# Hybrid SSD/MLA/PEER layer on one core: the modulation slabs' sums one unit later with two accumulators, TensorE's scan loop written out, and block 0's closing norm placed among block 1's expert rows

## The reference, cut to what matters

```python
ada = silu(c) @ w_ada + b_ada                       # (1, 6 * 2048), the modulation vector
shift1, scale1, gate1, shift2, scale2, gate2 = split(ada, 6)
h = layer_norm(x) * (1 + scale1) + shift1
z, xbc, dt_raw, q_a, kv_a, k_r, g_logits = split(h @ w_in)
y_ssd = ssd_branch(z, xbc, dt_raw, ...)             # 8 groups of 8 heads, scan in chunks of 64
y_mla = mla_branch(q_a, kv_a, k_r, ...)             # 16 heads, then one projection w_mla_out
mix = (g0 * y_ssd + g1 * y_mla) @ w_mix_out
x = post_layer_norm(ALPHA * x + (1 + gate1) * mix)
h2 = layer_norm(x) * (1 + scale2) + shift2
f = peer_ffn(h2, ...)                               # per token 8 heads x 16 experts of 16384
return post_layer_norm(ALPHA * x + (1 + gate2) * f)
```

## Time and profile before

| | us |
|---|---|
| median of 3 runs | 2916.93 (2910.3 to 2918.87) |
| the profiled execution's own time | 2912.79 |
| its span, first to last instruction | 2911.1 |
| TensorE busy | 2407.8 (83%) |
| DVE busy | 2123.8 (73%) |
| ACT busy | 982.4 (34%) |
| GpSimd busy | 881.9 (30%) |
| mean granted TensorE clock | 0.908 |
| mla, first to last matmul of its units | 424 to 533 |
| scan, eight groups | 535 to 1110 |
| last value row added | 2882.2 |

### The profile page before, as it was taken

The page is one execution under the profiler, slowest core; times in us unless marked ns, Lnnn a source line. Parts: engine busy times, 40 slices in busy tenths (PEclk is TensorE's granted clock), DMA queues, the critical chain, the costliest instruction groups (busy, mean ns, idle before and its releaser), DMA issues.

```text
span 2911.1 us, 38817 instructions
## 1 busy us (share of the span) xinstructions
PE 2407.8 (83%) x14598; PEld 2031.0 (70%) x14598; DVE 2123.8 (73%) x2562; ACT 982.4 (34%) x1337; POOL 881.9 (30%) x725
## 2 busy tenths in 40 slices
PE   4589998999999999999869766665565679999990
PEld 3589998988888888999759765665565664444440
DVE  7766667788878785444565888888898796666568
ACT  1144442344444444433343222225767630000000
POOL 0000001122222220000100565665665715444343
PEclk9799999999999999999989887877777779999995
DMA  8755658756555564655544899998999929999995
GB/s 343 290 171 200 226 198 295 254 203 205 203 201 202 203 210 167 233 179 182 217 144 145 339 368 377 397 376 361 394 374 370 414 90 413 413 413 414 414 413 228
DMA packets 144961, 817.83 MB, mean 281 GB/s; under 512 B 16520, under 2 KB 21248, under 8 KB 70832
## 3 DMA queue, kind: packets, MB, share of 16 engines
q0 software_dynamic: 93200, 477.21, 42.1%
q1 hardware_dynamic: 49728, 336.05, 31.3%
q10 hardware_dynamic: 1888, 2.59, 0.2%
HBM read 811.55 MB, written 4.23 MB: 280 GB/s over the span
## 4 chain that ended last, share of the span: by engine, by line
PE 42%; DVE 21%; DMA 20%; issue 9%; POOL 4%; ACT 3%; ACTq 0%; DVEq 0%; POOLq 0%
DMA vrow<-in_p_vg,acc 11%; PE ps L653 10%; PE ps L655 9%; PE ps L654 9%; DMA rrow<-in_peer_u,acc 7%; DVE ps L2042 3%; DVE rrow L2013 3%; POOL rrow L2177 3%; DVE wlo L1464 2%; ACT whi L1058 2%; PE ps L633 2%; DVE acc L1513 2%; PE ps L634 2%; PE ps L635 2%; DVE oh L2055 1%
## 5 line engine op out<-in xcount | busy, mean ns | idle before, releaser
L1464 DVE TENSOR_TENSOR wlo<-raw,whi 128x2048 fp32r<-128x2048 f32 x216 | 506.8, 2348 | 374.5 <-ACT whi L1058 365.1
L1058 ACT ACTIVATE whi<-raw 128x2048 fp32r<-128x2048 f32 x216 | 412.7, 1913 | 704.6 <-PE ps L655 479.2
L2177 POOL DMA_INDIRECT rrow<-in_peer_u,acc x256 | 443.5, 1732 | 455.4 <-DVE acc L1961 202.8
L2013 DVE CUSTOM_DVE_ANT_0 rrow<-rrow,h 128x2048 f32<-128x2048 f32 x200 | 449.6, 2287 | 61.0 <-DMA rrow<-in_peer_u,acc 60.6
L653 PE MATMUL ps<-h_hi,whi 128*128 128x256 f32 (+1 forms) x1568 | 453.1, 289 | 5.1 <-DVE wlo L1464 3.9
L2042 DVE SCALAR_TENSOR_TENSOR ps<-vrow,acc,ps 128x1024 f32<-128x1024 f32 x254 | 327.1, 1288 | 164.4 <-DMA vrow<-in_p_vg,acc 143.5
L654 PE MATMUL ps<-h_lo,whi 128*128 128x256 f32 (+1 forms) x1568 | 443.4, 283 | 0.0
L655 PE MATMUL ps<-h_hi,wlo 128*128 128x256 f32 (+1 forms) x1568 | 443.4, 283 | 0.0
L2177 POOL DMA_INDIRECT vrow<-in_p_vg,acc x256 | 247.7, 968 | 321.7 <-DVE ps L2042 232.6
L653 PEld LDWEIGHTS ps<-h_hi,whi 128*128 128x128 f32 (+1 forms) x1568 | 299.0, 191 | 17.9 <-issue 9.3
L654 PEld LDWEIGHTS ps<-h_lo,whi 128*128 128x128 f32 (+1 forms) x1568 | 299.0, 191 | 4.0 <-issue 3.8
(11 more groups left out here) (336 smaller groups left out, 4430.1 us busy)
## 6 DMA issues: line engine op xcount, KB each, us to landing
raw<-in_p_in SPq DMA_DIRECT2D x104, 1024.0 KB, 4.9
ada_in<-in_p_ada POOLq DMA_DIRECT2D x128, 512.0 KB
vden<-in_p_vd SPq DMA_DIRECT2D x64, 1024.0 KB
ada_in<-in_p_ada SPq DMA_DIRECT2D x32, 1024.0 KB, 10.0
raw<-in_p_so SPq DMA_DIRECT2D x32, 1024.0 KB, 4.8
raw<-in_p_mo SPq DMA_DIRECT2D x16, 1024.0 KB, 6.9
raw<-in_p_bc SPq DMA_DIRECT2D x16, 1024.0 KB, 4.9
raw<-in_p_mix SPq DMA_DIRECT2D x16, 1024.0 KB, 4.8
```

Of the source, the lines that this page charges most:

```text
L1058: F(whi[:, n % 2, :, 0:cols_], raw[:, n % 4, :, 0:cols_], ACT.Copy).then_inc(hi_ready, 1)
L1464: V.tensor_tensor(wlo[:, n % 2, :, 0:cols_], raw[:, n % 4, :, 0:cols_], whi[:, n % 2, :, 0:cols_].bitcast(F32), ALU.subtract).then_inc(lo_ ...
L2013: last = V.tensor_tensor_reduce(row, row, h2[:, b, :], 1.0, 0.0, ALU.mult, ALU.add, dots[:, k, e:e + 1])
L2177: return G.indirect_dma_start(out=dst, out_offset=None, in_=table, in_offset=bass.IndirectOffsetOnAxis(ap=eid_all[:, r:r + 1], axis=0))
```

## The change

- mla is written out on TensorE and ACT and DVE, as four slabs. DVE fills accumulator `s % 2`; TensorE sums slab s-1 after the first unit of slab s, and DVE makes the row after `lo(4s+2)`. Only the last slab's sum stays right behind its own units. ACT's store and bias load go behind the second split of the slab.
- In the scan the accumulator is `g`; TensorE sums the group before after unit u, DVE makes its row after `lo(u+2)`. Quarter 2 of the modulation sum goes from between `lo(u+8)` and `lo(u+9)` to behind the masks `mt`, ahead of `lo(u+10)`. GpSimd's list is as before.
- TensorE's scan is written out in Python, all four pairs; DVE, ACT and GpSimd keep their loops.
- The last group's sum, row and store go into g0's first units.
- The end: `residual(b, c)` makes one half of a block's residual and its two statistics, `last_norm(b)` the norm in two halves. Block 0's two halves stand before rows 192 and 236, its norm before row 240, block 1's dense half before row 246 (rows counted from 0 to 255). After the last row are left block 1's gathered half, its moments and its norm. SP stores four pieces of 512 KB.

```diff
 # SP
-                    sp_.wait_ge(fin_ready, b + 1)
-                    sp_.dma_start(out[0, b * P:(b + 1) * P, :], fin[:, b, :]).then_inc(out_done, 16)
+                    for c in range(0, D, DV):
+                        sp_.wait_ge(fin_ready, 2 * b + c // DV + 1)
+                        sp_.dma_start(out[0, b * P:(b + 1) * P, c:c + DV], fin[:, b, c:c + DV]).then_inc(out_done, 16)
 # PE, mla
-                with pe.Fori(0, 2) as i:
-                    pe.wait_ge(row_ready, i * 2 + (ADA_MLA + 1))
-                    for s in range(2):
-                        for q in range(4):
-                            pe.wait_ge(o_split, q + 1)
-                            channel_unit(U_MLA, 4 * s + q, i, N_MLA, oT_hi, oT_lo, 4 * q, DC - 1, slab_tiles(1 - s))
-                        if s:
-                            pe.wait_ge(row_ready, i * 2 + (ADA_MLA + 2))
-                        sum_slab(aux[:, 0, :], 0, i * 2 + (ADA_MLA + s))
+                pe.wait_ge(row_ready, ADA_MLA + 1)
+                for s in range(4):
+                    for q in range(4):
+                        pe.wait_ge(o_split, q + 1)
+                        channel_unit(U_MLA, 4 * s + q, 0, 0, oT_hi, oT_lo, 4 * q, DC - 1, slab_tiles(1 - s % 2))
+                        if s and q == 0:
+                            if s > 1:
+                                pe.wait_ge(row_ready, ADA_MLA + s)
+                            sum_slab(aux[:, 0, :], (s - 1) % 2, ADA_MLA + s - 1)
+                pe.wait_ge(row_ready, ADA_MLA + 4)
+                sum_slab(aux[:, 0, :], 1, ADA_MLA + 3)
 # PE, scan
                             channel_unit(U_SSD, u + q, i, N_SSD, h_hi, h_lo, 4 * q, DC - 1, slab_tiles(bx))
+                            if q == 0 and grp:
+                                sum_slab(aux[:, 2, :], 1 - g, grp - 1 + ADA_SSD)
...
-                        sum_slab(aux[:, 2, :], 0, grp + ADA_SSD)
...
-                ssd_pair(0, True)
-                with pe.Fori(1, 4) as i:
-                    ssd_pair(i, False)
+                for i in range(4):
+                    ssd_pair(i, i == 0)
 # ACT, mla
+                for s in range(4):
+                    for q in range(4):
+                        hi(U_MLA, 4 * s + q + 2, 0, 0)
+                        if q == 1:
+                            if s:
+                                ada2_store(ADA_MLA + s - 1)
+                            ada2_bias(ADA_MLA + s)
+                ada2_store(ADA_MLA + 3)
 # DVE
-                    dve.wait_ge(acc_summed, slab + (QUARTERS + 2))
+                    two = in_ssd or isinstance(slab, int) and slab > ADA_MLA
+                    dve.wait_ge(acc_summed, slab + (QUARTERS + 2) - (1 if two else 0))
...
+                for s in range(4):
+                    for q in range(4):
+                        ada2(ADA_MLA + s, q, into=s % 2)
+                        lo(U_MLA, 4 * s + q + 2, 0, 0)
+                        if s and q == 0:
+                            ada2_row(aux[:, 0, :], ADA_MLA + s - 1)
+                    slab_done(U_MLA, 4 * s + 3, 0, 0)
...
                         lo(U_SSD, u + 2, i, N_SSD)
+                        if not (first and g == 0):
+                            ada2_row(aux[:, 2, :], slab - 1)
                         lo(U_SSD, u + 3, i, N_SSD)
...
                         lo(U_SSD, u + 8, i, N_SSD)
-                        ada2(slab, 2, True)
                         lo(U_SSD, u + 9, i, N_SSD)
...
+                        ada2(slab, 2, True, g)
                         lo(U_SSD, u + 10, i, N_SSD)
-                        ada2(slab, 3, True)
+                        ada2(slab, 3, True, g)
                         lo(U_SSD, u + 11, i, N_SSD)
...
-                        ada2_row(aux[:, 2, :], slab)
 # DVE, the end
+                def residual(b, c, acc_):
+                    link(V.scalar_tensor_tensor(fin[:, b, c:c + DV], gate2b[:, c:c + DV], 1.0,
+                                                acc_.rearrange("p a n -> p (a n)"), ALU.add, ALU.mult))
+                    link(V.scalar_tensor_tensor(fin[:, b, c:c + DV], x1b[:, b, c:c + DV], ALPHA, fin[:, b, c:c + DV],
+                                                ALU.mult, ALU.add))
+                    for k in range(c // W, c // W + DV // W):
+                        S.step(V.bn_stats(bn[:, b, k, :], fin[:, b, k * W:(k + 1) * W]))
...
+                late = BLK * SEL - 64
                 for r in range(OHB // 4, BLK * SEL):
+                    if r == late:
+                        dve.wait_ge(last_in, 16 * 5)
+                        residual(0, DV, ps[:, 0, :, :])
+                    if r == late + 44:
+                        dve.wait_ge(vden_used, NVU)
+                        residual(0, 0, aux[:, 0:2, :])
+                        moments(0)
+                    if r == late + 48:
+                        last_norm(0)
+                    if r == late + 54:
+                        residual(1, 0, aux[:, 2:4, :])
                     add_row(r)
+                dve.wait_ge(vrow_used, BLK * SEL)
+                residual(1, DV, ps[:, 1, :, :])
+                moments(1)
+                last_norm(1)
```

More of the change, by code:

```diff
@@ L1609, in ada2 @@
                         dve.wait_ge(ada2_full[j % 4], slab * 32 + 16 * (j // 4 + 1))
[L1610 removed]
+                    last = ada_rows_in(acc[:, into, :], ada2_in[:, 2 + e if in_ssd else j % 4], 4 * q + 2 * e, 2)
                     if j == 7:
@@ new lines, in last_norm @@
+                def last_norm(b):
+                    rsqrt(st[:, 46 + 4 * b:47 + 4 * b], 17 + b)
+                    for c in range(0, D, DV):
+                        link(V.scalar_tensor_tensor(fin[:, b, c:c + DV], fin[:, b, c:c + DV], st[:, 44 + 4 * b:45 + 4 * b],
+                                                    ln2[:, 0, c:c + DV], ALU.subtract, ALU.mult))
+                        V.scalar_tensor_tensor(fin[:, b, c:c + DV], fin[:, b, c:c + DV], st[:, 46 + 4 * b:47 + 4 * b],
+                                               ln2[:, 1, c:c + DV], ALU.mult, ALU.add).then_inc(fin_ready, 1)
```

68 lines of the change are left out of this document (15 added, 53 removed).

## The result

| | before | after |
|---|---|---|
| median of 8 runs, us | 2914.2 (2910.3 to 2918.9) | 2923.3 (2918.6 to 2928.7) |
| ratio to before | 1 | 1.0035, 95% interval 1.0022 to 1.0047 |
| profiled execution, us (its span) | 2912.8 (2911.1) | 2922.0 (2920.4) |
| last sum of mla on TensorE, us from the start | 534.49 | 522.92 |
| that sum to the first hole behind the scan ("scan length") | 612.6 | 637.3 |

The forecast was +3.0 us with a range from -24 to +14; measured are +9.1. It runs from TensorE's last modulation sum of mla to a hole of 1.36 to 1.38 us in the projection behind the scan that every version has (at 1147.13 before, at 1160.24 after), so the scan alone has lost 24.7 us in these two executions.

What follows compares the result with a forecast made beforehand. TensorE was taken to bound the projections, transfers and DVE the expert stages behind them. Mla -10.8, scan +17.3 and end -3.5 made +3.0 us on the 2916.9 median: 2919.9, taken as 2920, range 2893 to 2931.

Steps and rivals of the forecast that it cites:

- Mla, -10.8 forecast: Attention projection: three 1.71 us holes, the 3.46 us hole and the slow unit's 2.2 us go; bounds 7 to 11 us.
- The scan, +17.3 forecast: Scan: seven periods cost 13.3 us more, the first boundary 2.0 and the clock at the last 2.0.
- The stall of 2.0 us: Scan, DVE ahead of quarter 3: it waits 2.0 us for the reload, issued only after quarter 2 is consumed.
- four masks 2.4: Scan, step in DVE's chain after the split of u+9 and the copy of cbm: the masks take 2.4 us.
- the 3.5 to 4.5 that I had named as the sign of being right: Scan, profile after: a hole of 3.5 to 4.5 us ahead of each group's third unit, ended by wlo.
- The end, -3.5 forecast: After the last rows: 25.0 us against 28.8, some tenths going to links; 3.5 us less, 1 to 5 at the ends.
- The clock, 2.0 us a boundary: Scan: TensorE's lower clock behind each new hole of 3.9 us costs 2.0 us each time.
- Rival 2: Scan: the clock doesn't fall at the new hole, saving 8 x 2.0 us; -13 us, 2904; chance 0.07.
- Rival 1: Scan: quarter 3's reload lands under 3.3 us, no stall, hole 1.9 us; about -24 us, 2893; chance 0.17.
- Rival 3: Scan: quarter 3's reload lands late, at 6.15 us, each boundary 0.85 later; +9.8 to +13 us, about 2928; chance 0.18.
- The loop written out, nothing beside the hole: TensorE's scan loop: writing it out is worth nothing, as its two holes are inside the 72.2 us period.
- every hole over 2.25 us: TensorE in the profiled stages: every hole over 2.25 us was followed by the lower clock; argued against an undiminished clock.

Runs made afterwards that it cites:

- no_reload: Changed kernel without GpSimd's load of quarter 3 in the scan, DVE adding quarter 2's rows again instead: 2906.8 us, -8.0 to the kernel before.
- q2_back: Changed kernel with quarter 2 of the scan's modulation sum moved back between the splits of u+8 and u+9: 2894.3 us, -19.4 to the kernel before.
- halves: Changed kernel with quarter 2's first half ahead of the split of u+9 and its second half behind it: 2892.7 us, -22.1 to the kernel before.
- q3_late: Changed kernel with quarter 2 split around u+9's split, quarter 3 behind the y output, row and TensorE's sum a unit later: 2875.0 us, ratio 0.9870 to before.
- The filler: Changed kernel with 32 idle matmuls behind unit u+1 of each group from the second on: 2909.8 us, -5.0 to the kernel before.
- scan_loop: Changed kernel with TensorE's scan loop as in the kernel before: 2921.9 us, +6.9 to the kernel before.
- end_only: Kernel before with only the change's end (output in halves, block 0's work among block 1's last rows): 2910.0 us, -3.7 to the kernel before.
- q2_back_loop: Changed kernel with quarter 2 at its old place and TensorE's scan loop as in the kernel before: 2901.5 us, -13.5 to the kernel before.
- only_q2: Kernel before with only quarter 2 of the scan's modulation sum moved behind the four masks: 2934.0 us, +20.3 to the kernel before.

## Why the prediction came out as it did

The time lies in the range (2893 to 2931), 3 us above the forecast in itself and 6 as a difference to before (the forecast started from the 2916.9 of three runs, and eight give 2914.2; the closer agreement is luck), and +0.35% is on the slower side of the 0.3% bound, for which I had given 0.27 and for "same" 0.47. Mechanism and signs of all three terms were right:

- **Mla, -10.8 forecast.** The profile shows 11.6, the run alone 11.8. The fear that transfers or ScalarE's store would give some back did not come true.
- **The scan, +17.3 forecast, +24.7 in the profile.** This is the term that was mis-sized. The stall of 2.0 us was right in its sum (2.07), in part by luck: I had the first half landing 5.3 us after its issue (ends 4.8 and 5.8) and the second behind it at no cost, while the first took 3.8 to 4.5 us to DVE's start and the second, 4.9 to 6.1, held DVE again. Mis-sized was "four masks 2.4": I took their duration from rows in which GpSimd's product had ended (658.81 + 2.94 = 661.75, masks from 664.35 on), while the edit itself moves them to before its end. The masks take 3.63 to 3.65 us in all eight groups of the changed kernel and of no_reload, and 2.48 to 2.50 in all eight of the kernel before, q2_back, halves and q3_late, where they start behind the product. These 1.2 us account for the 1.1 by which the chain is longer than forecast, and a period is 74.96 and not 74.1 us: 7 x 0.86 = 6.0, and 1.3 more at the first boundary. So the holes are 4.69 to 5.62 us, outside the 3.5 to 4.5 that I had named as the sign of being right.
- **The end, -3.5 forecast.** About 3 by the timeline, 3.7 by the run alone.
- **The clock, 2.0 us a boundary.** The filler gives 13.6 / 7 = 1.9. Rival 2, that the clock would not fall, is refuted: it is 0.69 to 0.78 behind each of the eight holes. Its price, 8 x 2.0 = 16 us, fits the 13.6 that seven of them gave back.
- **Rival 1, the reload in time,** is refuted: the two loads of group 1 took 3.96 and 5.38 us from issue to use, and of 50 modulation loads of the scan the profile has

```profile
DMA to landing us min/median/max: 3.4/4.8/6.3
```

  The rule of the Trainium skill ("DMA: Bandwidth & Descriptors", section "Anatomy of one DMA — SWDGE (gpsimd) path") gives an estimate of 3.2 us for these 512 KB, under the shortest; by it DVE would not have waited at 663.82 or 666.91, and the trace does not agree. And rival 1 priced a load in time too high: with no load at all a hole of 2.6 us and more stays (no_reload), where I had said 1.9. Without the load the time is 17 us under the changed kernel's; rival 1 stood 27 under the forecast.
- **Rival 3, the reload late,** was half right: the second half comes as late as 6.1 us after its issue (group 0), but the first never later than 4.5, and DVE's stand is 2.07 us on average. The extra time came from the masks instead.
- **The loop written out, nothing beside the hole:** right for this change (scan_loop), but worth 2 to 6 us as soon as the hole is gone. The parts are not additive: alone mla -11.8, end -3.7 and quarter 2 +20.3 make +4.8; against q2_back, which has the loop's gain, quarter 2 costs 28.5.

## What to carry to other kernels

When work is moved back on an in-order engine, ask what its buffers feed: the load that it releases may now be needed almost at once, while the early place hid it. Look for a stand of the same engine that can take the *follower* (here 3.15 us behind the y output), rather than put the mover back; that turned a loss of 9 us into a gain of 41. And when an edit moves an instruction in time, take its duration from rows in which its new neighbours run, not from its old place: here one move made quarter 2 shorter by 2.7 us and the masks longer by 1.2.

## What the runs showed of the hardware

- **Vector engine beside GpSimd.** Four masks (two operands each) take 2.50 us behind GpSimd's product and 3.65 when they start 1.9 us before its end; they start 5.8 us before quarter 3's load is issued, so it isn't that transfer. The four instructions of quarter 2 take 5.89 us beside GpSimd's multiplications and 3.21 without. GpSimd's product takes 2.94 us beside quarter 2 and 4.54 beside the split of u+9; halves, whose masks start 1.3 us after the product's end, shows the same 4.54, so it isn't the masks that lengthen it. The Trainium skill ("GPSIMD Engine Reference", section "1. Specifications") says that GpSimd's SBUF interfaces are shared with the vector engine, with contention for its instructions with two SBUF inputs; the trace agrees.
- **The clock behind holes of about 2 us.** One and the same hole is followed by the lower level or not. The windows of halves over two third units, behind holes of 1.93 and 2.02 us, and of q2_back over two units behind holes of 2.61 and 1.94:

```profile
675.77:682.00 6.23, 6.23 (x39) 6.23 (x40) 5.39 (x6) 0.02 (x1) 0.60 (x1) 0.73 0.76 278
748.21:754.00 5.79, 5.79 (x48) 5.79 (x49) 5.38 (x6) 0.00 (x0) 0.59 (x1) 1.00 0.78 268
```

```profile
729.80:735.40 5.60, 5.59 (x25) 4.63 (x26) 5.60 (x8) 0.00 (x0) 0.00 (x0) 1.00 0.94 343
656.57:663.00 6.43, 6.43 (x21) 5.17 (x22) 6.39 (x9) 0.07 (x1) 0.00 (x0) 0.73 0.87 308
```

  Behind 1.94 us the clock fell and behind 2.61 it did not; the prediction's "every hole over 2.25 us" is so in the kernel before and isn't in q2_back. no_reload's hole of 2.60 us was followed by a fall, too. The holes of 4 us and more in these scans were all followed by one.
- **A jump back on TensorE** shows stands from 0.72 us (end_only) over 1.11 and 1.58 (the kernel before) and 1.75 (q2_back_loop) to 3.02 (scan_loop) and 3.25 (only_q2), with the same loop. The profile puts the 1.58 down to DVE's split, which ended last there, and the others named to nothing that it shows. Why they differ is open.
